# Gate columns loaded outside the weight ring, a final norm by token halves, and an opening in chunks

## What is computed

```
h = rmsnorm(x, norm_gain[0])                    # opening
proj = h @ w_in_ab                              # 1024 x 4104
qa, ka, va, ga, qb, kb, vb, gb, fb = split(proj)   # eight of 512, fb of 8
ya = moba_attention(norm(qa), norm(ka), va)     # 8 heads of 64, with distance slopes
log_f = log_sigmoid(fb + b_forget)              # 8 heads x 256 tokens
c = cumsum(log_f)                               # fox: score(i, j) += c[i] - c[j]
yb = fox_attention(norm(qb), norm(kb), vb, log_f)
x = x + concat(ya * silu(ga), yb * silu(gb)) @ w_out_ab
...
x = x + square(relu(h @ mlp_w_in)) @ mlp_w_out  # last layer
return x * rsqrt(mean(x * x) + eps) * norm_final
```

## Time and profile before

| | us |
|---|---|
| runs (three): median, lowest, highest | 1068.36, 1067.81, 1068.61 |
| the profiled execution, whole | 1072.39 |
| its span, first to last instruction | 1070.6 |
| PE, DVE, ACT, POOL busy | 1001.8, 637.2, 544.5, 42.4 |
| mean granted TensorE clock | 0.967 |

### The profile page before, as it was taken

One profiled execution on the slowest core, in us unless ns is written; L12 is line 12 of the kernel. 1 busy time (PEld: TensorE's weight loads), 2 busy tenths in 40 slices (PEclk: granted clock), 3 DMA queues, 4 the chain that ended last, 5 costly groups with the idle time before them and its releaser, 6 DMA issues.

```text
span 1070.6 us, 15661 instructions
## 1 busy us (share of the span) xinstructions
PE 1001.8 (94%) x6152; PEld 889.3 (83%) x6152; DVE 637.2 (60%) x1202; ACT 544.5 (51%) x1015; POOL 42.4 (4%) x80
## 2 busy tenths in 40 slices
PE   6998899999798988997999999999999989999996
PEld 5877778786686878986899999899988869999995
DVE  4867855484855465745775555556873657654552
ACT  5466564464565344635654444454673456444351
POOL 2110400000111000000000000000000000000000
PEclk9999899999888999999999999999999989999998
DMA  7966313554322334442366555656435415555650
GB/s 244 256 122 156 109 50 112 165 172 143 116 82 69 75 98 115 157 135 102 120 196 193 176 184 195 236 159 191 148 102 188 157 45 193 185 182 186 196 177 39
DMA packets 117685, 158.61 MB, mean 148 GB/s; under 512 B 17814, under 2 KB 59116, under 8 KB 117612
## 3 DMA queue, kind: packets, MB, share of 16 engines
q1 hardware_dynamic: 117612, 157.61, 47.9%
HBM read 156.55 MB, written 1.05 MB: 147 GB/s over the span
## 4 chain that ended last, share of the span: by engine, by line
PE 81%; DVE 7%; ACT 5%; issue 3%; DMA 2%; SPq 1%; POOL 1%; DVEq 0%; POOLq 0%; ACTq 0%
PE bank L464 24%; PE bank L465 23%; PE bank L466 23%; PE bank L596 2%; DMA raw<-in_w_in_ab 2%; DVE w_lo L1581 2%; PE bank L621 2%; PE bank L610 2%; PE bank L518 2%; ACT pb L1289 1%; ACT w_hi L1160 1%; SPq L2210 1%; PE bank L630 0%; DVE nl L1763 0%; PE bank L581 0%
## 5 line engine op out<-in xcount | busy, mean ns | idle before, releaser
L1581 DVE TENSOR_TENSOR w_lo<-raw,w_hi 128x1024 fp32r<-128x1024 f32 (+3 forms) x300 | 343.4, 1190 | 194.4 <-ACT w_hi L1160 194.0
L1160 ACT CAST w_hi<-raw 128x1024 fp32r<-128x1024 f32 (+3 forms) x300 | 289.9, 1025 | 158.9 <-DMA raw<-in_mlp_w_in 73.9
L464 PE MATMUL bank<-xT_hi,w_hi 128*128 128x256 f32 x792 | 226.2, 286 | 2.7 <-DVE xT_lo L1631 1.8
L466 PE MATMUL bank<-xT_hi,w_lo 128*128 128x256 f32 x792 | 224.3, 283 | 0.0
L465 PE MATMUL bank<-xT_lo,w_hi 128*128 128x256 f32 x792 | 224.3, 283 | 0.0
L464 PE MATMUL bank<-w_hi,xT_hi 128*128 128x512 f32 (+1 forms) x432 | 165.0, 382 | 6.0 <-DVE w_lo L1581 3.7
L465 PE MATMUL bank<-w_lo,xT_hi 128*128 128x512 f32 (+1 forms) x432 | 161.0, 373 | 0.0
L466 PE MATMUL bank<-w_hi,xT_lo 128*128 128x512 f32 (+1 forms) x432 | 160.6, 372 | 0.0
L464 PEld LDWEIGHTS bank<-xT_hi,w_hi 128*128 128x128 f32 x792 | 152.2, 192 | 4.4 <-issue 2.6
L465 PEld LDWEIGHTS bank<-xT_lo,w_hi 128*128 128x128 f32 x792 | 152.2, 192 | 0.6
L466 PEld LDWEIGHTS bank<-xT_hi,w_lo 128*128 128x128 f32 x792 | 152.1, 192 | 0.0
(11 more groups left out here) (218 smaller groups left out, 1085.0 us busy)
## 6 DMA issues: line engine op xcount, KB each, us to landing
raw<-in_mlp_w_in SPq DMA_DIRECT2D x32, 1024.0 KB, 5.3
raw<-in_mlp_w_out SPq DMA_DIRECT2D x32, 1024.0 KB, 5.1
raw<-in_w_in_ab SPq DMA_DIRECT2D x16, 1024.0 KB, 11.4
raw<-in_w_in_cd SPq DMA_DIRECT2D x13, 1024.0 KB, 5.1
raw<-in_xa_w_kv SPq DMA_DIRECT2D x8, 1024.0 KB, 4.9
raw<-in_sb_w_qkv SPq DMA_DIRECT2D x16, 512.0 KB, 5.1
raw<-in_w_out_ab SPq DMA_DIRECT2D x4, 1024.0 KB, 5.1
raw<-in_w_out_cd SPq DMA_DIRECT2D x4, 1024.0 KB, 5.1
```

The source lines that it names most:

```text
L464: pe.matmul(o, wh, ih, start=start, stop=False, skip_group_check=True)
L466: return pe.matmul(o, wl, ih, start=False, stop=stop, skip_group_check=True)
L1160: nc.scalar.copy(w_hi[:, u % SLOTS, a], raw[:, u % SLOTS, a]).then_inc(hi_ready, 1)
L1581: V.tensor_tensor(w_lo[:, u % SLOTS, a], raw[:, u % SLOTS, a], w_hi[:, u % SLOTS, a].bitcast(F32), ALU.subtract).then_inc(lo_ready, 1)
```

## The change

There are three parts.

1. The opening. The gain rows are issued first, then x by column halves instead of token halves. Units 0, 1 and 2 are loaded, cast and subtracted in four pieces each (PIECED = 3, 256 KB a piece, one semaphore each), interleaved with the chunks of x's transposes, each of which has a bank of its own for the left half. PE goes through these units chunk by chunk, both token halves in each. Six matmuls on the identity (`warm`) stand ahead. Unit 5 is issued ahead of the small loads, which are four instead of seven.
2. The gate columns. Unit f leaves the ring. One DMA loads the 8 columns (128 x 8 x 8 elements) into `f_raw` behind unit 4; ACT and DVE split them. The result has 8 rows. foxL and foxR are gone: POOL makes a small selection matrix `pick`, PE multiplies it with c and a row of ones in `fox_rows` (step 6), which puts c and the ones in two rows for each head, at rows 0, 32, 64 and 96, and ACT and DVE copy the two banks. The second product of a fox head's scores is over 2 rows.
3. The tail. The last `down` takes both units for token half 0 and then both for token half 1. Residual, gain, square, rsqrt and scaling run for each token half; the last scaling is shared by ACT (left columns, its own output DMA) and DVE (right columns, SP's DMA).

```diff
-    add(("f", 0), KC * P, (0, KC, 8, P, rows(ab)[:, :, f0:f0 + 8]),
-        *((c, KC, 32, P, rows(ab)[:, :, f0 - 24:f0 + 8]) for c in (8, 40, 72)), (104, KC, 24, P, rows(ab)[:, :, 0:24]))
...
-                for t, (a, z) in enumerate(k["spans"]):
-                    keys = z - a
+                if k["kind"] == "fox":
                     for n, (q, kk) in enumerate(zip(k["parts"], k["keys"])):
-                        ins = pe.matmul(banks[b][:, a:z], q(t * P, (t + 1) * P), kk(0, keys),
-                                        start=n == 0, stop=n == len(k["parts"]) - 1)
+                        for t, (a, z) in enumerate(k["spans"]):
+                            ins = pe.matmul(banks[b][:, a:z], q(t * P, (t + 1) * P), kk(0, z - a),
+                                            start=n == 0 and t == 0, stop=n == 1, skip_group_check=True)
...
+            def warm(n):
+                for _ in range(n):
+                    pe.matmul(banks[7][:, 0:P], ident[:, :], ident[:, :], start=True, stop=True)
...
+                for one in range(T * 4):
+                    t, c = (one % T, one // T) if by_chunk else (one // 4, one % 4)
...
+            def fox_rows():
+
+                pe.wait_ge(pick_ready, 1)
+                pe.wait_ge(fox_sums, 1)
+                for side in range(2):
+                    begin(("fox", side), side)
+                    for j in range(2):
+                        ins = pe.matmul(banks[side][:, j * S:(j + 1) * S], pick[:, 2 * side + j, :], fox_c, start=True, stop=True)
+                    end(("fox", side), ins, (fox_ready, 1 + side))
...
-                5: [unit("vb", 0), turn("kb", 5, 1)], 6: [unit("vb", 1)], 7: [unit("gb", 0)], 9: [unit("gb", 1)],
+                5: [unit("vb", 0), turn("kb", 5, 1)], 6: [unit("vb", 1), fox_rows], 7: [unit("gb", 0)], 9: [unit("gb", 1)],
...
+            def start():
+
+                first = ("n", 0)
+                split_piece(0, 0)
+                hi_one((first, 0), 0, xT_hi, in_bank=1)
+                hi_one((first, 0), 1, xT_hi, in_bank=1)
+                for c in range(1, 4):
+                    split_piece(0, c)
+                    if c < 3:
+                        hi_one((first, 0), c + 1, xT_hi, in_bank=1)
+                for c in range(4):
+                    split_piece(1, c)
+                for t in range(T):
+                    x_squares(first, 0, t, (x_left_in, 16))
+                for c in range(4):
+                    hi_one((first, 1), c, xT_hi, 4)
+                    split_piece(2, c)
...
+                act.wait_ge(fox_in, 16)
+                own.sig(nc.scalar.copy(f_hi[:, :, :], f_raw[:, :, :]), fox_split)
...
-            for t in range(T):
-                sp.dma_start(x[:, t, :], tok(A["x"])[:, t, :]).then_inc(x_in, 16)
             gain_rows(*gain_loads[0])
-            for u in range(SLOTS):
+            sp.dma_start(x[:, :, 0:PANEL], tok(A["x"])[:, :, 0:PANEL]).then_inc(x_left_in, 16)
+            pieces(0)
+            pieces(1)
+            sp.dma_start(x[:, :, PANEL:], tok(A["x"])[:, :, PANEL:]).then_inc(x_right_in, 16)
+            pieces(2)
+            for u in range(PIECED, SLOTS):
                 weight(u)
+            sp.dma_start(f_raw[:, :, :], f_cols).then_inc(fox_in, 16)
             for load in gain_loads[1:]:
                 gain_rows(*load)
+            weight(SLOTS)
             sp.wait_ge(setup_ready, 1)
```

The tail's new code on DVE, for t = 0 and 1:

```diff
+                for n in range(2):
+                    a = slice(n * PANEL, (n + 1) * PANEL)
+                    ps = condition(dve, ("d", 1, n, t))
+                    own.sig(V.scalar_tensor_tensor(out=x[:, t, a], in0=ps[:, :], scalar=rs2(("p", 1), t), in1=x[:, t, a], op0=ALU.mult, op1=ALU.add), x_ready)
+                    own.settle()
+                    own.sig(V.tensor_tensor(xn[:, t, a], x[:, t, a], final_gain[:, a], ALU.mult), gained_ready)
...
+                dve.wait_ge(gained_ready, 2 * t + 2)
+                own.sig(V.tensor_scalar(xn[:, t, PANEL:], xn[:, t, PANEL:], rstd[:, c:c + 1], None, ALU.mult), out_right_ready)
```

314 lines of the change are left out of this document (204 added, 110 removed).

## The result

The changed kernel takes 1065.49 us in the median of 22 runs (1057.81 to 1069.49), the kernel before 1070.89 us beside it (22 runs, 1063.64 to 1077.28): ratio 0.9941, interval 0.9921 to 0.9962, 6.3 us faster (4.1 to 8.5; the two medians lie 5.4 apart). A second comparison gave 0.9940 (0.9916 to 0.9965). The forecast was a gain of 12.9 us, a time of 1055.5 and a range of 1050.0 to 1062.0: the sign was right, the gain about half of it, the time outside.

What follows compares the result with a forecast made beforehand. PE was taken as the bound, busy 1001.8 of 1070.6 us, so only its gaps and low-clock stretches count. 3.6 + 4.7 + 5.6 - 2.0 - 1.0 + 2.0 = 12.9 us off 1068.36 gave 1055.5, range 1050.0 to 1062.0.

Steps and rivals of the forecast that it cites:

- The opening: Up to the first scores: chunked loading and an earlier unit 5 start them 3.6 us sooner, bounds 1.0 and 5.0.
- The first: Opening: the gate columns delay unit 5, only 0.5 us of the keys' wait stays gained; time 1058.6, chance 0.14.
- The second: Waits removed at 90 to 120 us partly return, half of 4.7 + 5.6 stays; time 1060.7, chance 0.15.
- The third: More than forecast: unit 5 fully earlier, no memory charge, fox scores overlapping; time 1050.5, chance 0.10.
- The fourth: Opening: pieces of 256 KB move at half rate, scores 0 come 5 us later; time 1064.1, chance 0.05.
- the fifth: Units 0 to 4: gaps in chunked supply keep PE from 2.4 GHz; slower, up to 1075.1, chance 0.02.
- The keys' wait: First scores: PE's 1.16 us wait for scaled keys goes because POOL's fill of foxL is gone; 1.2 us.
- The gate unit: First 120 us: f out of the ring removes three PE waits and a half-clock stretch; 4.7 us, bounds 2.5 and 5.
- foxL and foxR: Before the first fox head: the 2.97 us table wait and the slow stretch behind it go; 5.6 us, bounds 3.5 and 6.
- Scores of the fox heads: Fox heads' four products: fewer contracted rows change nothing, or gain up to 0.35 us per head if parts overlap.
- Memory statistics: Around heads 7 and 8: ACT's passes over mem and DVE's scaling cost 1.0 us, bounds 0 and 2.
- Tail: After the last product: finishing by token halves with scaling shared by ACT and DVE gains 2.0 us, bounds 1 and 3.

Runs made afterwards that it cites:

- f_late: The changed kernel with the gate columns' DMA issued behind unit kb 1 instead of unit 4, the columns split in pipeline steps 2 and 3; 1058.2 us, ratio 0.9869.
- the second trace: The changed kernel as it is, run and profiled once more; 1065.2 us, ratio 0.9940 to the kernel before.
- part_opening: The kernel before with the new opening alone, no gate columns loaded there, gate unit, foxL, foxR and tail as before; 1064.7 us, ratio 0.9944.
- fill_late: part_opening with POOL's filling of foxL started behind the first scores instead of the first transposes of qa; 1063.2 us, ratio 0.9923 to the kernel before.
- f_late_64: f_late with the gate sums laid out so that a fox head's second product covers the same 64 rows as its first; 1055.5 us, ratio 0.9849.

## Why the prediction was right and wrong

**The opening (3.6, bounds 1.0 and 5.0; measured -1.05).** This is the step that failed. "Unit 5 is 0.2 to 2.4 us earlier; I take 1.2": it came 3.1 us later. The price of the gate columns' DMA was taken from the earlier trace rows as 0.4 us if only issued and 2.6 if it has to drain, and set against 2.8 us of small loads. With the weights of the opening outstanding its issue took 2.70 us here, and the first gain load behind it 6.09 where 2.55 are enough without it; it landed 12.2 us after issue where 3.5 had been read from a quiet stretch. The prediction's sum looked only at this DMA and at the small loads. The gain rows stayed between it and unit 5, so that 5.6 of these 6.1 us reached unit 5 (issued at 28.49, in f_late at 22.87). Two neighbours were right: the pieces (first product 7.83 for 7.3, high clock from 13.09, in the second trace from 8.2) and what is late next (DVE's chain behind unit 5). With the DMA elsewhere the first scores come 4.7 us before; the charge of 0.7 us for short waits wasn't needed, and unit 5 is cast 2.0 us earlier for the 1.2 taken.

**The rivals.** The first, "the gate columns delay unit 5", was the mechanism, at 0.14, with the price again too low: it kept 0.5 us for the opening and gave 1058.6. The second (half of 4.7 + 5.6 stays away) is refuted in the one trace, with 9.2 of 10.3 us gained, and less clearly in the other, with 7.6. The third failed with unit 5 and with the fox scores, which cost instead of overlapping. The fourth (pieces at half rate) is refuted by part_opening, the fifth by the spacing of 0.23 us from 13.1 us on.

**The keys' wait (1.2 of the 3.6).** Right in cause, as fill_late shows; its worth rose from 1.16 to 3.7 us as PE came sooner.

**The gate unit (4.7, bounds 2.5 and 5; measured 5.15).** Right: the three waits are gone, and the granted clock of 95 to 100 is 1.00 for 0.66.

**foxL and foxR (5.6; measured 4.0 in one trace, 2.4 in the other).** The wait for the table is gone as said. The clock behind it isn't back: PE runs at 0.50 from 116 to 118 us in the one trace and from 116 to 122 in the other, without a wait, and the bounds (3.5 to 6) took it for given that the slow stretch was the wait's. The prediction had named a clock of 0.5 between 60 and 120 us as a sign of being wrong, and it is one.

**fox_rows (-2.0; measured -1.92)** right. **Scores of the fox heads (nothing, or a gain; measured -1.6)**: the argument by column counts left out what a change of rows costs. The -2.0 us of the whole stage (-4.1 in the second trace) are more than that: the wait of 2.04 us at 149.60 is gone, but PE works 10 us at half clock where it had been some 3. **Memory statistics (-1.0; measured 0)**: no wait appeared, in f_late_64 with its faster scores none either ahead of 140.27. **Tail (2.0; measured 2.3)** right by the rows.

**The base.** The median of three runs, 1068.36, lies 2.5 to 4 us below those of 11 to 35 runs of the same kernel (1070.9 to 1072.3). Of the 10 us between forecast and result 2.5 are the base's and 7.5 the gain's (5.4 by the two medians for 12.9).

Taken together the forecast of 12.9 us is nearly what f_late gives (13.6 and 14.2 by medians, with a mean clock up by 0.003 to 0.005; 12.3 by the stages of its trace). The sum was that of a kernel in which the gate columns don't stand ahead of unit 5. That it fits f_late so well is partly luck: 1.1 us more in the opening, 0.5 at the gate unit, 0.3 in the tail and 1.0 not lost at the memory statistics stand against 1.6 less from the table wait and 2.0 lost at the fox heads.

## What to carry to other kernels

Price an added transfer where it will stand, not where it was seen, and look at what is issued behind it: the same DMA held its queue for 0.5 us at 53 us, and in the opening it and the load behind it held it 6 to 7 us longer than that load alone. Moving it a few places back, behind unit 5, moved the wait and not the time; what helped was to take it out of the stretch in which loads are the bound, and nothing used its columns before. And compare parts with the whole: where the ratios of the parts multiply to less than the whole shows, two parts may share a resource, and the rows have to say which.

A pair of profiles compares two executions. Sum stage by stage only where the change acts, and leave out what moves in stages it doesn't touch.

## What the runs showed of the hardware that I had not expected

- A change between products over 64 and over 32 or fewer rows costs PE 0.19 to 0.20 us (1.57, 1.77, 2.15 us for two, three and five changes), which made the two-row operand dearer than the forty-row one. Zeros up to 64 rows took the cost away.
- A DMA's issue isn't short when much is outstanding: behind five units it took 6.99 us for 32 KB and, in the kernel before, 7.55 us for 8 KB, against 0.41 us for 1 MB at 28.49. The size of the DMA that is issued doesn't decide it.
- The granted clock fell to 0.50 for 10 us, 139 to 149, though PE had had no wait of 0.5 us or more for 95 us.
- Two executions of one kernel differ by up to 11.7 us (1057.8 to 1069.5) along with the granted clock, and filling seven waits with small products raised the clock of their stretch from 0.89 and 0.93 to 0.98 without a gain in time.
